# Modulation chunks moved into the feed-forward loops, and a new order in sparse attention

## The reference

```
cond = silu(c)
mod = cond @ ada_w[i] + ada_b[i]                    # 1024 x 9216 for each layer
sh0, sc0, g0, sh1, sc1, g1, sh2, sc2, g2 = split(mod, 9)
h = rmsnorm(x, pre_norm) * (1 + sc) + sh
y = sublayer(h)                                     # swiglu(1024 -> 2752 -> 1024) or attention
x = x + (0.5 or 1) * g * rmsnorm(y, post_norm)
```

```
q, k, v, qi, ki, wi = split(h @ w_in)               # 16 heads of 64 on one k and v; 8 index heads
score = sum over index heads of wi * relu(qi . ki), causal
keep the 64 keys with the highest score of each query
p = softmax(q . k / 8 over the kept keys);  y = (p @ v) @ w_out
```

## Time and profile before

| | us |
|---|---|
| median of 3 runs | 2064.28 |
| lowest and highest run | 2063.08, 2071.99 |
| profiled execution | 2064.1 |
| its span in the profile | 2062.4 |

### The profile page before, as it was taken

How to read it: one execution, slowest core, us unless ns; L and a number is a source line. 1 busy time by engine, 2 the same in 40 slices (tenths; PEclk the granted TensorE clock), 3 DMA queues, 4 the chain that set the end, 5 groups by cost and what they waited for, 6 DMA issues and landing times.

```text
span 2062.4 us, 30508 instructions
## 1 busy us (share of the span) xinstructions
PE 1957.2 (95%) x12303; PEld 1654.1 (80%) x12303; DVE 1275.1 (62%) x1781; ACT 973.8 (47%) x1380; POOL 68.1 (3%) x152
## 2 busy tenths in 40 slices
PE   8999999989899999997999988999999999789998
PEld 7888787869588888876999843799989989658997
DVE  3763454536699889897555575555565565645554
ACT  4555411214477777764333444433443345464333
POOL 6000000000000000000000000000000000000000
PEclk9999999989899999998999999999999999899999
DMA  9893432116989999993555688365556546135553
GB/s 309 312 311 123 163 103 82 42 54 237 397 313 352 343 325 343 366 352 124 185 188 177 247 348 346 123 225 183 163 200 206 186 153 216 51 112 164 184 183 102
DMA packets 207726, 442.95 MB, mean 215 GB/s; under 512 B 8237, under 2 KB 158957, under 8 KB 184065
## 3 DMA queue, kind: packets, MB, share of 16 engines
q1 hardware_dynamic: 201584, 424.70, 59.4%
q0 software_dynamic: 6032, 16.74, 2.5%
HBM read 440.21 MB, written 1.20 MB: 214 GB/s over the span
## 4 chain that ended last, share of the span: by engine, by line
PE 70%; DVE 6%; ACT 4%; issue 1%; DMA 0%; SPq 0%; ACTq 0%; DVEq 0%
PE P L761 69%; ACT merged L1681 1%; DVE w_lo L2280 1%; DVE xs L2233 1%; DVE h L2233 1%; PE P L1369 0%; ACT w_hi L1713 0%; ACT proj L1681 0%; ACT st L1681 0%; DMA ring<-in_w_gate 0%; PE P L1493 0%; DVE st L2607 0%; ACT pT L1681 0%; ACT h L1681 0%; DVE xs L2226 0%
## 5 line engine op out<-in xcount | busy, mean ns | idle before, releaser
L761 PE MATMUL P<-x_parts,w_hi 128*128 128x256 f32 x2560 | 458.5, 281 | 2.2 <-DVE w_lo L2280 2.2
L2280 DVE TENSOR_TENSOR w_lo<-ring,w_hi 128x1024 fp32r<-128x1024 f32 x302 | 351.7, 1219 | 87.0 <-ACT w_hi L1713 86.8
L761 PEld LDWEIGHTS P<-x_parts,w_hi 128*128 128x128 f32 x2560 | 397.0, 188 | 9.2 <-DVE w_lo L2280 2.9
L761 PE MATMUL P<-w_hi,x_parts 128*128 128x256 f32 (+2 forms) x1504 | 374.8, 336 | 7.7 <-DVE w_lo L2706 4.5
L761 PE MATMUL P<-x_parts,w_lo 128*128 128x256 f32 x1280 | 359.5, 281 | 0.0
L1713 ACT ACTIVATE w_hi<-ring 128x1024 fp32r<-128x1024 f32 x302 | 297.8, 1051 | 58.0 <-DMA ring<-in_ffn_w_down 46.8
L2706 DVE TENSOR_TENSOR w_lo<-ring,w_hi 128x1024 fp32r<-128x1024 f32 x240 | 280.3, 1221 | 28.8 <-ACT w_hi L1951 26.2
L761 PEld LDWEIGHTS P<-w_hi,x_parts 128*128 128x128 f32 x1504 | 258.8, 191 | 45.7 <-issue 13.3
L1951 ACT ACTIVATE w_hi<-ring 128x1024 fp32r<-128x1024 f32 x240 | 240.5, 1052 | 86.4 <-DMA ring<-in_w_up 30.8
L761 PEld LDWEIGHTS P<-x_parts,w_lo 128*128 128x128 f32 x1280 | 241.1, 188 | 0.0
L761 PE MATMUL P<-w_lo,x_parts 128*128 128x256 f32 (+2 forms) x752 | 234.9, 334 | 0.0
(11 more groups left out here) (508 smaller groups left out, 2635.9 us busy)
## 6 DMA issues: line engine op xcount, KB each, us to landing
ring<-in_ada_w SPq DMA_DIRECT2D x72, 1024.0 KB, 7.5
ring<-in_ffn_w_gate SPq DMA_DIRECT2D x44, 1024.0 KB, 5.5
...
```

The source lines that it names most:

```text
L761: return pe.matmul(o, l, r, start=start, stop=stop, **kw)
L2280: dve.tensor_tensor(w_lo[:, slot, c:c + half], ring[:, slot, c:c + half], w_hi[:, slot, c:c + half].bitcast(F32), ALU.subtract).then_inc(s ...
```

## The change

**Modulation.** The ring keeps the 20 units of chunks 0 to 4 of layer 0: 4 behind the gate step, 16 behind the mixer. The 20 units in the projections and all units of layer 1 in sparse attention are gone from it. The other 13 chunks of 1024 columns are computed in the four feed-forward sublayers (`MOD_CHUNKS`): four in each of the first three, one for each round of the loop, and one in the last. SP loads a chunk in four units of 256 rows into `mod_w`, which has four slots, between the loads of the ring. DVE multiplies and adds them (`mod_step`, two instructions before each `hidden`), starting from the bias; PE sums over the 128 partitions with four matmuls (`sum_chunk`) at the end of the round, ACT copies the sum (`chunk_out`) and POOL stores it.

**Sparse attention.** The three units with k, v, index queries, index key and weights are loaded and projected first. The index transposes stand behind step 8 of 14 of the projection, the index products behind steps 10 and 11, in six parts of a whole bank with one relu of 512 columns each. DVE does index scores and selection of tile 0 behind the rotary step of the index part, before the rotary steps of the queries. The rounds of tile 1 stand behind units 0 and 1, and the gains of the next sublayer ahead of the index scores. ACT drains the second projection tile before it turns to the normed columns, and copies units three ahead; this holds for differential attention too.

```diff
-ADA_UNITS, ADA_QUADS = 36, 5
-QUAD_UNITS = [list(range(8 * q, 8 * q + 8)) if q < 4 else [32, 33, 34, 35] for q in range(ADA_QUADS)]
-QUADS = (2, 3, 4, 0, 1), (4, 0, 1, 2, 3)
-BANKS = (6, 7, 6, 0, 1), (7, 6, 7, 6, 7)
-EARLY = 3
-ADA_ORDER = [[k for q in quads for k in QUAD_UNITS[q]] for quads in QUADS]
-EARLY_ADA = sum(len(QUAD_UNITS[q]) for q in QUADS[0][:EARLY])
-NEXT_ADA = len(QUAD_UNITS[QUADS[1][0]])
-PROJ_PLACES = {"sparse": [0, 1, 2, 4, 6, 8, 10], "differential": list(range(12))}
-WOVEN = {2: 0, 3: 1, 4: 2, 5: 3, 6: 4}
-DRAINS = [(0, k) for k in range(EARLY)] + [(1, 0)] + [(0, k) for k in range(EARLY, ADA_QUADS)] + [(1, k) for k in range(1, ADA_QUADS)]
+ADA_CHUNKS = 5
+ADA_UNITS, ADA_QUADS = 20, 3
+QUAD_UNITS = [list(range(8 * q, 8 * q + 8)) if q < 2 else [16, 17, 18, 19] for q in range(ADA_QUADS)]
+QUADS = 2, 0, 1
+BANKS = 7, 0, 1
+EARLY = 1
+ADA_ORDER = [k for q in QUADS for k in QUAD_UNITS[q]]
+EARLY_ADA = sum(len(QUAD_UNITS[q]) for q in QUADS[:EARLY])
+MOD_CHUNKS = {0: [(0, 5), (0, 6), (0, 7), (0, 8)], 2: [(1, 0), (1, 1), (1, 2), (1, 3)], 3: [(1, 4), (1, 5), (1, 6), (1, 7)], 5: [(1, 8)]}
+MOD_SLOTS = 4
...
-for n in reversed(range(EARLY_ADA)):
-    _put([s for s in STEPS if s[0] == "proj"][2 + n * 16 // EARLY_ADA], [("ada", n)])
...
+STEPS += [("d_gate",), ("b_pre",)] + [("ada", n) for n in range(2)]
+STEPS += [_MERGE[8]] + [("ada", n) for n in range(2, EARLY_ADA)] + [_MERGE[9], ("d_attn",), _MERGE[10], ("d_intra",)]
...
                     in_units = out[first:]
-                    del out[first:]
-                    for u, load in enumerate(in_units):
-                        out.append(load)
-                        if u in WOVEN:
-                            ada(1, NEXT_ADA + WOVEN[u])
-                    for n in range(NEXT_ADA + len(WOVEN), ADA_UNITS):
-                        ada(1, n)
+                    out[first:] = in_units[4:] + in_units[:4]
...
+            mod_after = {}
+            for m, chunks in MOD_CHUNKS.items():
+                first = marks[m // 3, m % 3 // 2]
+                for j in range(4 * len(chunks)):
+                    mod_after.setdefault(first + R + 3 * j // 2, []).append((m, j))
+            def load_mod(m, j):
+                u = 4 * chunks_ahead(m) + j
+                if j < MOD_SLOTS:
+                    sp.wait_ge(sem("gu"), 22 * sorted(MOD_CHUNKS).index(m) + 2)
+                if u >= MOD_SLOTS:
+                    sp.wait_ge(sem("mod_used"), 2 * (u - MOD_SLOTS + 1))
+                sp.dma_start(mod_w[:, u % MOD_SLOTS, :, :], mod_source(A, *MOD_CHUNKS[m][j // 4], j % 4)).then_inc(sem("mod_unit%d" % (u % MOD_SLOTS)), 16)
             for n, load in enumerate(loads):
+                for m, j in mod_after.get(n - 1, ()):
+                    load_mod(m, j)
...
+            def sum_chunk(r, c0):
+                pe.wait_ge(sem("mod_used"), r * 8 + (8 * c0 + 8))
+                for j in range(4):
+                    x = mm(P[32 * j:32 * j + 1, 3, 0:256], ones[:, 0:1], mod_sum[:, 256 * j:256 * j + 256])
+                x.then_inc(sem("ada_used"), 1)
...
             def ffn(n):
                 n0, h0 = unit[0], tiles_before[0]
                 first_tiles(n, n0, h0)
-                with pe.Fori(0, 4) as r:
+                c0, chunks = chunks_ahead(n), len(MOD_CHUNKS[n])
+                if chunks < 4:
+                    four_tiles(n0 + 6, 0, h0 + 4)
+                    sum_chunk(0, c0)
+                with pe.Fori(chunks % 4, 4) as r:
                     four_tiles(n0 + 6, r, h0 + 4)
+                    if chunks == 4:
+                        sum_chunk(r, c0)
...
+                steps(0, 8)
                 t.see("roped")
                 for i in range(2):
                     turns([proj[:, i, 1152 + 128 * k:1280 + 128 * k] for k in range(4)])
-                t.see("dup")
-                for i in range(2):
-                    turns([dup[:, i, :], dup2[:, i, :]])
+                turns([dup2[:, i, :] for i in range(2)])
+                steps(8, 10)
                 pe.wait_ge(sem("turned"), t.sent["turn"])
-                n = 0
-                for i in range(2):
-                    kw = 128 * (i + 1)
-                    if i:
-                        turns([proj[:, 1, 128 * k:128 * k + 128] for k in range(8)])
-                    for hh in range(8):
-                        r = slice(64 * (hh % 2), 64 * (hh % 2) + 64)
-                        if n >= 2:
-                            pe.wait_ge(sem("idx_relu"), n - 1)
-                        x = mm(P[:, n % 2, 0:kw], qiT[r, hh // 2, i * 128:i * 128 + 128], kT[r, 1, 0:kw])
-                        t.tell(x, "idx")
-                        n += 1
-                    fill((4, 2)[i])
+                for part in range(4):
+                    index(part)
+                steps(10, 11)
+                pe.wait_ge(sem("idx_relu"), 2)
+                for part in (4, 5):
+                    index(part)
+                steps(11, 14)
+                unit[0] += len(SPARSE_COLS)
+                def turn_queries(i):
+                    t.see("roped")
+                    turns([proj[:, i, 128 * k:128 * k + 128] for k in range(8)])
+                    turns([dup[:, i, :]])
+                    pe.wait_ge(sem("turned"), t.sent["turn"])
+                turn_queries(0)
...
                 scores(0)
                 scores(1)
+                turn_queries(1)
                 for n, (i, hg) in enumerate(units):
                     if n + 2 < len(units):
                         scores(n + 2)
-                    fill(2 if i else 3)
                     t.see("p_ready")
...
+            def chunk_out(r, c0):
+                act.wait_ge(sem("ada_used"), r + (ADA_UNITS + c0 + 1))
+                act.wait_ge(sem("ada_stored"), r * 16 + 16 * (ADA_QUADS + c0 + 1))
+                act.activation(ada_row[:, 0:256], P[:, 3, 0:256], ACT.Copy).then_inc(sem("ada_out"), 1)
...
                     project_out(n + 1, 0)
+                    project_out(n + 1, 1)
                 columns(n + 1, 1)
...
+                units = len(project_cols[SUBLAYERS[sub]])
+                high(unit[0], (2,))
                 for k in range(2 * units):
-                    if ahead == 3 and k % 2 == 0:
-                        high(unit[0], (places[k // 2 + 3],))
-                    if k:
+                    if k % 2 == 0 and k // 2 + 3 < PROJ_UNITS_OF[SUBLAYERS[sub]]:
+                        high(unit[0], (k // 2 + 3,))
+                    if k > 1:
                         project_out(sub, k)
-                    if ahead == 2 and k % 2 == 0 and 3 <= k // 2 + 2 < units:
-                        high(unit[0], (places[k // 2 + 2],))
+                    if k in behind:
+                        behind[k]()
...
+                a_project(n, {7: index_columns, 9: lambda: relu(range(4)), 10: lambda: relu((4, 5))})
...
+            def mod_step(k, r, c0):
+                dve.wait_ge(sem("mod_unit%d" % k), r * 16 + 16 * (c0 + 1))
+                if k == 0:
+                    dve.wait_ge(sem("ada_out"), r + (ADA_QUADS + c0))
+                    dve.wait_ge(sem("modr_here"), r * 16 + 16 * (c0 + 3))
+                else:
+                    dve.wait_ge(sem("mod_used"), r * 8 + (8 * c0 + 2 * k))
+                one, two = (cols[:, V_C + 2 * k + t:V_C + 2 * k + t + 1] for t in range(2))
+                dve.scalar_tensor_tensor(out=mod_sum, in0=mod_w[:, k, 0, :], scalar=one, in1=mod_sum if k else mod_bias,
+                                         op0=ALU.mult, op1=ALU.add).then_inc(sem("mod_used"), 1)
+                dve.wait_ge(sem("mod_used"), r * 8 + (8 * c0 + 2 * k + 1))
+                dve.scalar_tensor_tensor(out=mod_sum, in0=mod_w[:, k, 1, :], scalar=two, in1=mod_sum,
+                                         op0=ALU.mult, op1=ALU.add).then_inc(sem("mod_used"), 1)
...
+                c0, chunks = chunks_ahead(n), len(MOD_CHUNKS[n])
+                if chunks == 4:
+                    out_gain(n, "ffn")
+                else:
                     for k in range(4):
+                        mod_step(k, 0, c0)
+                        hidden(k, 0, h0 + 4)
+                        low(n0 + 6, AFTER[k])
+                with dve.Fori(chunks % 4, 4) as r:
+                    for k in range(4):
+                        if chunks == 4:
+                            mod_step(k, r, c0)
                         hidden(k, r, h0 + 4)
                         low(n0 + 6, AFTER[k], r)
...
             def v_sparse(sub):
-                low(unit[0], PROJ_PLACES["sparse"][2:])
-                dve.wait_ge(sem("proj_out"), proj_before[0] + 10)
-                for i in range(2):
-                    apply_rope(i, 0, 17)
-                v.mark("roped")
-                dve.wait_ge(sem("proj_out"), proj_before[0] + 14)
-                proj_before[0] += 14
+                low(unit[0], (2, 3, 4))
+                dve.wait_ge(sem("proj_out"), proj_before[0] + 6)
                 for i in range(2):
```

(33 more changed lines are left out.)

366 lines of the change are left out of this document (191 added, 175 removed).

## The result

The changed kernel takes 2038.34 us, median of four runs (2035.96 to 2041.57), beside 2066.49 for four runs of the kernel before, measured together with it: ratio 0.9865, 95% interval 0.9845 to 0.9885. Six more runs of the same kernel, measured at a later time, gave 2043.39, ratio 0.9895 (0.9876 to 0.9915), 5 us more than the first four. The forecast was 2041.1 with a range of 2025 to 2058. The profiled execution took 2041.57 us, its span is 2039.9 (before 2062.4), so the trace has to explain 22.5 us.

The account below looks back on a forecast made before the run. PE bounds projections and feed-forward loops, a chain of engines sparse attention; 2064.1 - 14.0 (projections) + 6.4 (chunks) - 14.4 (sparse) - 1.0 (differential) = 2041.1 us, range 2025 to 2058.

Parts of the forecast that it names:

- Projections, -14.0 forecast: Projections: removing 20 modulation units frees 22.3 us of PE, waits for DVE give 8.3 back; bounds -22.3 and -9.
- the two long waits for low halves: Projections: PE waits for low halves that DVE finishes late, 2.4 us at one unit and 1.9 at a later one.
- Chunks, +6.4 forecast: Feed-forward loops: 13 added chunks cost PE 0.49 us each; DVE steps, ACT copies and loads cost nothing.
- term of 0.49 a chunk: Feed-forward loops: four 256-column matmuls per chunk take half the 0.97 us of four 512-column ones.
- The step "with 7 us of slack": Feed-forward loops: DVE's first step of a chunk waits under 1 us for ACT's copy, with 7 us of slack.
- Rival 3: Feed-forward loops: chunk chain or SyncE waits exceed 7 us of slack, PE waits each chunk; 2093 at 4 us; chance 0.06.
- Sparse, -14.4 forecast: Sparse attention: -15.2 from earlier masked rows, -3.6 from removed fills, +2.7 and +1.7 for TensorE's clock; ends -19 and -5.
- The order's part: Sparse attention: work moved beside the query units brings the first masked rows 15.2 us earlier.
- The fills' part: Sparse attention: without modulation matmuls between the attention's steps, DVE and ACT wait less, saving 3.6 us at full clock.
- The output projection's start: Sparse attention: the output projection starts at TensorE's low clock level, adding 1.7 us.
- rival 1: PE stays at 1.2 GHz through sparse attention, which then gives 5 us; sum 2050.5; chance 0.17.
- Differential, -1.0 forecast: Differential attention: PE's 1.92 us wait for the second projection tile's drain goes, the next drain holds PE about 0.9.

Follow-up runs that it names:

- units back: Changed kernel with the 20 modulation units put back in the projections, their sums read by nobody: 2053.1 us, ratio 0.9946 to the kernel before.
- work out: Changed kernel with taps 2 to 4 of the twelve convolutions left out: 2034.96 us, ratio 0.9853 to the kernel before.
- work reordered: Changed kernel with DVE's and ACT's steps of the projections in another order, nothing left out: 2038.47 us, ratio 0.9874 to the kernel before.
- the filled kernel: Changed kernel with unread 256-column matmuls put where PE waits in sparse attention: 2037.18 us, ratio 0.9877 to the kernel before.
- all together: Changed kernel with projection steps reordered further, ACT two units ahead in the sparse projection, and sparse attention's PE waits filled: 2034.26 us, ratio 0.9835.

## Why the prediction was right, and where it was off

The time is right, and partly by luck, since errors of several us cancel: the projections gave 2.1 us less than forecast, the chunks cost 3.2 more and one trace's start 2.9, while sparse attention gave 3.2 more and 4.2 came from places that the forecast did not touch.

**What bounds the kernel** stood: PE in the projections and the loops, DVE and then ACT in the sparse attention.

**Projections, -14.0 forecast, -11.9 measured.** The mechanism is shown from both sides (units back, work out, work reordered), and the two long waits for low halves came as worked out: 2.4 and 1.9 us forecast, 2.50 and 2.00 measured. Two sizes were off: the units took 23.4 us of PE, not 22.3 (the busy time of the earlier trace rows was the better price), and the waits, counted as 8.3 and measured at 8.1, brought two dips of the clock with them, 3.4 us that the sum had not.

**Chunks, +6.4 forecast, +9.6 measured.** The term of 0.49 a chunk was read from a chain of equal matmuls; between others the sum costs 0.74. Both ends of the range, 6.2 and 13, held. That the rest costs nothing was right for the loop as it is. The step "with 7 us of slack" looked at the wrong wait: it prices DVE's wait for ACT's copy and doesn't name the one of PE's sum for DVE's last multiply-add, whose slack is 1.25 us at the first chunk and was 0.41 at another. It cost nothing here, but one DVE instruction more a tile would have cost most of the gain. Rival 3 was nearer than 6 in 100 says, with another mechanism than the one I priced: a late DVE at the loop's entry.

**Sparse, -14.4 forecast, -17.6 and -19.6 measured.** The order's part, -15.2, was right to 0.1: the first masked rows start at 1199.88, 15.3 nearer to the sublayer's start. Its pieces hold too: from the end of the selection to these rows it is 9.7 us, where 9.6 was counted. DVE's first four units took 21.48 us (1199.88 to 1221.36) against 21.13. The fills' part has to be read together with the clock's: -3.6 and +2.7 were forecast; -0.6 is measured for both together in the kernel before, and +2.4 for the clock alone up to the output projection in the changed one, so that the fills alone come to some -3, an estimate across two kernels. Missing was ACT's drain, -1.3. The output projection's start was put at +1.7 and came at +0.7 and -1.5. Attention units of the second tile stand 5.4 us apart, and the granted clock was 0.52 in the first window and 0.80 in the second, where "below 0.8" was written.

**The rule of the Trainium skill** ("TensorE: Matmul & The Clock Gate", section "HAM oscillation — how this bites in real kernels") has its mechanism here: without fills the granted clock falls to 0.5 for 30.7 us. Its price is not what rival 1 made of it (9.4 us) but 2.6 to 4.6 in the sublayer by the filled kernel's trace, and nothing by the trace of all together beside the changed kernel's second. That it is small because most of the low stretch lies beside DVE's work (busy for 26.64 of the 30.7 us) is argued.

**Differential, -1.0 forecast, -1.3 measured.** PE's wait of 1.92 us became one of 0.99, as worked out. It was not tested apart, and the same code of the kernel before took 153.77, 154.83 and 154.76 us in three traces.
